# Eleven small parameter loads move from ScalarE's DMA queue to SyncE's, behind the first weight chunk, and TensorE runs five idle products instead of ten before x

## The chip, the cores and the metric

The kernel runs on one core of one Trainium2 chip. The metric is the device time of one execution in microseconds (us). Three runs of the kernel before took 1094.04 to 1094.62 us, median 1094.55 us. The profile is of one more execution, which took 1093.83 us.

Engines: PE is TensorE (PEld its weight loads), DVE is VectorE, ACT is ScalarE, POOL is GpSimd, SP is SyncE, which here only issues DMAs. ACT issues DMAs too, on a queue of its own.

## The reference

One layer of a hybrid encoder on 256 frames of 1024 numbers, all in float32. A normed copy of x is multiplied by `w_in`, and the product is split into a convolution branch, a state-space branch and two gates. After that comes a mixture of 32 experts, top 4 of each frame.

```python
h = rms_norm(x, norm_mix_g)
proj = h @ w_in                                   # 1024 x 3840
a_val, a_gate, u, g_conv, g_ssm = split(proj)
v = a_val * sigmoid(a_gate)
v = depthwise_causal_conv(v, conv_w) + conv_b     # 31 taps
y_conv = silu(layer_norm(v, conv_ln_g, conv_ln_b)) @ w_conv_out
y_ssm = s5_branch(u, ssm_a_re, ssm_a_im, ssm_log_step, b, c, ssm_d, w_ssm_glu, b_ssm_glu) @ w_ssm_out
x = x + (sigmoid(g_conv) * y_conv + sigmoid(g_ssm) * y_ssm) @ w_out
x = x + moe(rms_norm(x, norm_ffn_g))              # 32 experts: 1024 -> 2 x 1024 -> 1024
return rms_norm(x, norm_final_g)
```

The weights of all experts, some 400 MB, are read from HBM in every execution.

## The kernel before

Each engine has one program, written out in order; semaphores link them. The weights pass through a ring of 24 slots of 1 MB each in on-chip memory. SP issues every load of it in a fixed order, and before it fills a slot again it waits for the product that used the slot last. `w_in` comes in 15 chunks of 256 columns, the first one in two halves of 512 KB (L373, L374), the others whole (L369). After the mixer the ring holds the weights of two experts; each expert takes 12 slots, and its slots are filled again for the expert after next.

The start, with which the change deals, goes like this. SP issues x in two tiles of 128 frames (L362), then the gain of the first norm (L364, `norm_mix_g`, counted on the semaphore of x's second tile), then `w_in`. ACT issues eleven small loads at the same time: the convolution taps in two pieces (L648, semaphore `tap_in`), and nine rows or groups of rows of parameters (L649 to L654, semaphore `par_in`), all of them into rows of two on-chip tiles, `tap_rows` and `par_rows`. Then ACT loads the table for the square root (L656) and squares the two tiles of x (L659) for the norm's sums.

PE first multiplies the identity by itself ten times (L1367, `START_WARM`), into a bank that nobody reads. Then it transposes x's first tile, eight transposes (L1373), the gain (L1371), and x's second tile. DVE and ACT multiply the transposed x by the gain (L914, L665) into `hraw`. The first products with `w_in` (L1417 in `first_half`) run on this `hraw`, before the norm's divisor is known: four steps of k on the chunk's first half, then in the same instruction stream `spread_rstd` (two products, L1427, that spread the divisor over the partitions, and L1431, which transposes the 62 parameter rows), then four steps of k on the chunk's second half. L1431 waits for all nine parameter loads (`par_in`) and for a copy on POOL (L523) that itself waits for them. After `first_half` PE transposes the taps (L1466, waits for `tap_in`), and the rest of the projection follows (L1398), beside which DVE runs the convolution's taps.

PE issues in order: behind a waiting transpose everything else of PE waits. A float32 product stands in the trace as two instructions, so ten products are 20 records.

Of the kernel before, what the change touches and what calls it, by code (L numbers as in the profile page):

```python
# [33 lines left out]
W = 31  # L34
DS = 256
G, P, H = 16, 64, 16
ST = G * P // 128
# [21 lines left out]
MIDDLE = 4, 4, 4  # L59
END = {E - 3: (4, 2, 2, 2, 2), E - 2: (2, 2, 2, 2, 1, 1, 1, 1), E - 1: (2, 2, 2, 1, 1, 1, 1, 1, 1)}  # L60
WARM = 3, 4
START_WARM = 10
LEVELS = 8
BLOCK_STEPS = 16
AGAIN_STEPS = 6
# [4 lines left out]
def build(nc, x, norm_mix_g, w_in, conv_w, conv_b, conv_ln_g, conv_ln_b, w_conv_out,  # L70
# [3 lines left out]
    with ExitStack() as ctx:  # L74
# [3 lines left out]
        def sem(name):  # L78
            return ctx.enter_context(nc.semaphore(name))
# [4 lines left out]
        def at(slot, n, off=0):  # L84
            return ring[:, slot * CH + off:slot * CH + off + n]
# [98 lines left out]
        par_rows = ring[0:62, 12 * CH:12 * CH + 128]  # L184
        tap_rows = at(22, DC)[0:W, :]
# [22 lines left out]
        log_steps = ring[0:ST, 12 * CH + 1018:12 * CH + 1020]  # L208
# [6 lines left out]
        par_in = sem("par_in")  # L215
        tap_in = sem("tap_in")
# [143 lines left out]
        def _(sp):  # L360
# [5 lines left out]
            def load_win(c):  # L366
                if c >= WRING:
                    sp.wait_ge(win_pe, c - WRING + 1)
                sp.dma_start(grid(at(c % WRING, CH), KD, 256),  # L369
                             win_v[:, :, ORDER[c] * 256:ORDER[c] * 256 + 256]).then_inc(win_in[c % WRING], 16)  # L370

            win0, win0_v = grid(at(0, CH), KD, 256), win_v[:, :, ORDER[0] * 256:ORDER[0] * 256 + 256]
            sp.dma_start(win0[:, 0:4, :], win0_v[:, 0:4, :]).then_inc(win_in[0], 16)  # L373
            sp.dma_start(win0[:, 4:8, :], win0_v[:, 4:8, :]).then_inc(win0_late, 16)  # L374
            for c in range(1, WRING):
                load_win(c)
            for ri, src in enumerate((ssm_b_re, ssm_b_im)):
# [266 lines left out]
        def _(act):  # L644
            s = nc.scalar

            for r0, r1 in ((0, 16), (16, W)):
                act.dma_start(tap_rows[r0:r1, :], conv_w[0, r0:r1, :]).then_inc(tap_in, 16)  # L648
            act.dma_start(log_steps, ssm_log_step[0].rearrange("(t g) -> t g", g=2)).then_inc(par_in, 16)  # L649
            for src, r0 in ((ssm_a_re, 8), (ssm_a_im, 16)):  # L650
                act.dma_start(par_rows[r0:r0 + ST, :], src[0].rearrange("(t g) p -> t (g p)", g=2)).then_inc(par_in, 16)
            for src, r0, n in ((norm_ffn_g, 24, 8), (conv_b, 40, 6), (conv_ln_g, 46, 6), (conv_ln_b, 52, 6), (ssm_d, 58, 2),
                               (b_ssm_glu, 60, 2)):
                act.dma_start(par_rows[r0:r0 + n, :], src[0].rearrange("(k p) -> k p", p=128)).then_inc(par_in, 16)  # L654
            act.wait_ge(consts, 1)
            s.activation(neg_top, ident[:, 0:2], ACT.Sqrt)  # L656
            for t in range(TT):
# [705 lines left out]
        def _(pe):  # L1363
            mm, tr = nc.tensor.matmul, nc.tensor.transpose
            pe.wait_ge(consts, 1)
            for _ in range(START_WARM):
                mm(bank[6][:, 256:384], ident[:, :], ident[:, :], start=True, stop=True)  # L1367
# [496 lines left out]
```

## Time and profile before

| | |
|---|---|
| median of three runs | 1094.55 us |
| profiled execution | 1093.83 us |
| its span, first to last instruction | 1091.7 us |
| PE busy | 1054.1 us (97%) |
| DVE, ACT, POOL busy | 298.9, 151.3, 83.4 us |
| DMA engines, mean over the span | 395 GB/s |

The span leaves out 2.1 us of the profiled execution that lie before the first and after the last instruction. Times in the rows below are microseconds from the start of the span. In a row of the timeline, the first number is the start, the second how long the instruction or the run of like instructions took, and in brackets at the end stands how long the engine was idle before, and what ended that. "xN" is a count. A matmul's own duration includes its way through the array; how far apart the starts of two matmuls lie is the better measure of the rate.

### The profile page before, as it was taken

To read this page: it belongs to the slowest core of one execution; us is meant where nothing else is said; L and a number is where in the kernel's file an instruction comes from. 1 tells how busy PE (TensorE), PEld (TensorE's weight loads), DVE (VectorE), ACT (ScalarE), POOL (GpSimd) and SP (SyncE) were. 2 spreads that over 40 slices of the span, in tenths; PEclk is the share of its full clock that TensorE was granted. 3 is DMA by queue.
4 is the path that set the end of the run, shared out by engine and by line. 5 is a ranking of instruction groups with operands and counts; after the bars stand their busy time and mean duration, and the time that the engine had idled before them with its cause. 6 is when DMAs were issued, how large, how long until landed. Compare 5 with 4: busy or idle time off the path is not lost.

```text
span 1091.7 us, 12228 instructions
## 1 busy us (share of the span) xinstructions
PE 1054.1 (97%) x4978; PEld 456.8 (42%) x4979; DVE 298.9 (27%) x684; ACT 151.3 (14%) x276; POOL 83.4 (8%) x161
## 2 busy tenths in 40 slices
PE   9999999999999999999999999999999999999996
PEld 8888876333333333333333333333323333333332
DVE  5999843311111111111111111111111011111112
ACT  4111503101011111101010001100000000000003
POOL 3986100000000000000000000000000000000000
PEclk9999999999999999999999999999999999999999
DMA  9756786899999999999999999999999999999996
GB/s 284 232 167 256 316 349 255 343 428 434 430 430 435 430 433 431 432 432 432 431 433 431 428 431 428 435 430 432 432 432 432 432 430 433 431 433 424 425 424 249
DMA packets 43268, 431.48 MB, mean 395 GB/s; under 512 B 6773, under 2 KB 22443, under 8 KB 25482
## 3 DMA queue, kind: packets, MB, share of 16 engines
q1 hardware_dynamic: 42800, 430.48, 94.2%
q10 hardware_dynamic: 442, 0.64, 0.2%
q8 instruction: 18, 0.29, 0.1%
q14 instruction: 8, 0.07, 0.0%
HBM read 430.06 MB, written 1.05 MB: 395 GB/s over the span
## 4 chain that ended last, share of the span: by engine, by line
PE 71%; DMA 25%; ACT 1%; DVE 1%; issue 0%; another core or an unknown queue 0%; POOL 0%; SPq 0%; DVEq 0%; POOLq 0%
PE bank L1681 30%; DMA ring<-w_gate_up 23%; PE bank L1693 14%; PE bank L1398 9%; PE bank L1707 4%; PE bank L1619 3%; DMA ring<-w_down 3%; PE bank L1533 2%; PE bank L1561 2%; ACT area L788 1%; PE bank L1647 1%; PE bank L1672 1%; PE bank L1521 1%; PE bank L1575 1%; PE bank L1652 1%
## 5 line engine op out<-in xcount | busy, mean ns | idle before, releaser
L1681 PE MATMUL bank<-ring,area 128*64 128x512 f32 x2048 | 454.4, 600 | 18.8 <-DMA ring<-w_gate_up 18.8
L1681 PEld LDWEIGHTS bank<-ring,area 128*64 128x64 f32 x2048 | 149.9, 138 | 305.7 <-issue 268.4
L1693 PE MATMUL bank<-ring,area 128*64 128x512 f32 x1024 | 227.3, 595 | 5.6 <-ACT area L788 3.0
L1231 DVE TENSOR_SCALAR area<-bank 128x512 f32<-128x512 f32 x32 | 22.1, 692 | 668.6 <-PE bank L1681 668.6
L1693 PEld LDWEIGHTS bank<-ring,area 128*64 128x64 f32 x1024 | 71.7, 137 | 140.8 <-issue 132.9
L1398 PE MATMUL bank<-area,ring 128*128 128x256 f32 x464 | 102.3, 381 | 0.0
L1398 PEld LDWEIGHTS bank<-area,ring 128*128 128x128 f32 x464 | 87.5, 190 | 13.8 <-issue 1.8
L794 ACT ACTIVATE area<-area 128x512 f32<-128x512 f32 x32 | 20.1, 630 | 484.1 <-DVE area L1231 484.1
L1009 DVE SCALAR_TENSOR_TENSOR bank<-ring,spread,bank 128x256 f32<-128x256 f32 x174 | 71.5, 484 | 0.6
L1707 PE MATMUL bank<-area,spT 64*128 64x512 f32 x248 | 61.6, 615 | 0.7 <-ACT area L791 0.7
L1619 PE MATMUL bank<-rows,pick 128*64 128x512 f32 x256 | 62.2, 605 | 0.0
L791 ACT ACTIVATE area<-bank 128x512 f32<-128x512 f32 x32 | 19.1, 597 | 220.3 <-PE bank L1693 220.3
L1707 PEld LDWEIGHTS bank<-area,spT 64*128 64x128 f32 x248 | 21.3, 186 | 40.5 <-issue 38.9
L1647 PE MATMUL bank<-ident,area 128*128 128x128 f32 x256 | 36.8, 280 | 1.4 <-DVE area L1240 1.2
L1221 DVE TENSOR_TENSOR area<-bank,gain 128x512 f32<-128x512 f32 x31 | 21.4, 692 | 50.0 <-PE bank L1647 50.0
L1240 DVE TENSOR_TENSOR area<-area 128x512 f32<-128x512 f32 x32 | 34.2, 1067 | 1.1
L1619 PEld LDWEIGHTS bank<-rows,pick 128*64 128x64 f32 x256 | 15.5, 136 | 41.2 <-issue 41.0
L1647 PEld LDWEIGHTS bank<-ident,area 128*128 128x128 f32 x256 | 28.3, 141 | 5.8 <-DVE area L1240 1.5
L785 ACT ACTIVATE area<-bank 128x512 f32<-128x512 f32 x32 | 19.1, 598 | 75.8 <-PE bank L1619 75.8
L1237 DVE SCALAR_TENSOR_TENSOR area<-area 128x512 f32<-128x512 f32 x32 | 21.9, 685 | 0.0
L1234 DVE TENSOR_SCALAR area<-bank 128x512 f32<-128x512 f32 x32 | 21.8, 681 | 0.0
L1561 PE MATMUL bank<-ring 128*128 128x512 f32 x48 | 20.9, 592 | 0.0
(277 smaller groups left out, 513.4 us busy)
## 6 DMA issues: line engine op xcount, KB each, us to landing
ring<-w_gate_up SPq DMA_DIRECT2D x51, 4096.0 KB, 45.6
ring<-w_down SPq DMA_DIRECT2D x25, 4096.0 KB, 43.2
ring<-w_gate_up SPq DMA_DIRECT2D x26, 1024.0 KB, 8.8
ring<-w_gate_up SPq DMA_DIRECT2D x13, 2048.0 KB, 43.6
ring<-w_down SPq DMA_DIRECT2D x18, 1024.0 KB, 12.5
ring<-w_in SPq DMA_DIRECT2D x14, 1024.0 KB, 8.5
ring<-w_down SPq DMA_DIRECT2D x5, 2048.0 KB, 12.6
ring<-w_conv_out SPq DMA_DIRECT2D x1, 3072.0 KB, 13.1
```

The source lines that it names most:

```text
L1009: ins = v.scalar_tensor_tensor(conv[:, k, :] if w == W - 1 else acc, src, taps[:, k, w:w + 1], acc, ALU.mult, ALU.add)
L1231: return v.tensor_scalar(gc, bank[4][:, :], 7.0, None, ALU.min)
L1237: return v.scalar_tensor_tensor(lc, lc, 1.0, gc, ALU.add, ALU.mult)
L1240: return v.tensor_tensor(gc.rearrange("a (m p) -> a p m", p=128), grid(lc, 128, 4), grid(sg, 128, 4), ALU.mult)
L1398: last = mm(half_bank[n][m] if n < 2 else win_bank(n)[:, m * T:m * T + T], w[:, k, m * 128:m * 128 + 128], hT[:, k, :], start=(k == 0), st ...
L1533: last = mm(bank[4 + j][:, m * T:m * T + T], wconv[:, k, c:c + 128], silu[:, k, :], start=(k == 0), stop=(k == KC - 1))
L1561: return mm(bank[2 * t + h][:, :], gateC[:, k, t * 128:t * 128 + 128], wout[:, k, h * 512:h * 512 + 512], start=(k == 0), stop=(k == KD - 1))
L1619: last = mm(bank[6][64 * h:64 * h + 64, :], pick[:, t, :], rows[:, t, :].rearrange("a (p h m) -> a h p m", h=2, m=4)[:, h, :, :], start=(t ...
L1647: last = tr(bank[b][:, m * 128:m * 128 + 128], src[:, m * 128:m * 128 + 128], ident[:, :])
L1681: last = mm(bank[4 + b][64 * h:64 * h + 64, :], heT[:, k % 4, k // 4 * 64:k // 4 * 64 + 64], fours(w, b, h), start=False, stop=(k == KD - 1))
L1693: last = mm(bank[b][64 * h:64 * h + 64, :], src[:, k % 4, k // 4 * 64:k // 4 * 64 + 64], w[:, k % 2, h * 512:h * 512 + 512], start=(k == 0 ...
L1707: return mm(bank[n][:, :], by[r, n // 2, :], y[r, :], start=start, stop=stop, skip_group_check=True)
```

## The change

Two edits. The constant `START_WARM` goes from 10 to 5. And the eleven small loads are issued by SP, in the same order among themselves, after both halves of `w_in`'s first chunk and before its second chunk; ACT issues nothing at the start.

```diff
-START_WARM = 10
+START_WARM = 5
...
             sp.dma_start(win0[:, 0:4, :], win0_v[:, 0:4, :]).then_inc(win_in[0], 16)
             sp.dma_start(win0[:, 4:8, :], win0_v[:, 4:8, :]).then_inc(win0_late, 16)
+            for r0, r1 in ((0, 16), (16, W)):
+                sp.dma_start(tap_rows[r0:r1, :], conv_w[0, r0:r1, :]).then_inc(tap_in, 16)
+            sp.dma_start(log_steps, ssm_log_step[0].rearrange("(t g) -> t g", g=2)).then_inc(par_in, 16)
+            for src, r0 in ((ssm_a_re, 8), (ssm_a_im, 16)):
+                sp.dma_start(par_rows[r0:r0 + ST, :], src[0].rearrange("(t g) p -> t (g p)", g=2)).then_inc(par_in, 16)
+            for src, r0, n in ((norm_ffn_g, 24, 8), (conv_b, 40, 6), (conv_ln_g, 46, 6), (conv_ln_b, 52, 6), (ssm_d, 58, 2),
+                               (b_ssm_glu, 60, 2)):
+                sp.dma_start(par_rows[r0:r0 + n, :], src[0].rearrange("(k p) -> k p", p=128)).then_inc(par_in, 16)
             for c in range(1, WRING):
                 load_win(c)
...
-            for r0, r1 in ((0, 16), (16, W)):
-                act.dma_start(tap_rows[r0:r1, :], conv_w[0, r0:r1, :]).then_inc(tap_in, 16)
-            act.dma_start(log_steps, ssm_log_step[0].rearrange("(t g) -> t g", g=2)).then_inc(par_in, 16)
-            for src, r0 in ((ssm_a_re, 8), (ssm_a_im, 16)):
-                act.dma_start(par_rows[r0:r0 + ST, :], src[0].rearrange("(t g) p -> t (g p)", g=2)).then_inc(par_in, 16)
-            for src, r0, n in ((norm_ffn_g, 24, 8), (conv_b, 40, 6), (conv_ln_g, 46, 6), (conv_ln_b, 52, 6), (ssm_d, 58, 2),
-                               (b_ssm_glu, 60, 2)):
-                act.dma_start(par_rows[r0:r0 + n, :], src[0].rearrange("(k p) -> k p", p=128)).then_inc(par_in, 16)
             act.wait_ge(consts, 1)
             s.activation(neg_top, ident[:, 0:2], ACT.Sqrt)
```

The start of ACT's program before, from its first load to its first table; `ring` is the tile of 24 slots in which the parameter rows lie, and the two numbers are rows and columns:

```order
L648 DMA ring<-conv_w 16x768
L648 DMA ring<-conv_w 15x768
L649 DMA ring<-ssm_log_step 8x2
L651 DMA ring<-ssm_a_re 8x128
L651 DMA ring<-ssm_a_im 8x128
L654 DMA ring<-norm_ffn_g 8x128
L654 DMA ring<-conv_b 6x128
L654 DMA ring<-conv_ln_g 6x128
L654 DMA ring<-conv_ln_b 6x128
L654 DMA ring<-ssm_d 2x128
L654 DMA ring<-b_ssm_glu 2x128
L656 ACT_TABLE_LOAD
```

In the changed kernel none of these eleven loads is left on ACT, and the table load is its first work. SP's program of the changed kernel, from the row behind the first chunk's second half to the second chunk (line numbers are the changed kernel's; L369 is the same line in both):

```order
L376 DMA ring<-conv_w 16x768
L376 DMA ring<-conv_w 15x768
L377 DMA ring<-ssm_log_step 8x2
L379 DMA ring<-ssm_a_re 8x128
L379 DMA ring<-ssm_a_im 8x128
L382 DMA ring<-norm_ffn_g 8x128
L382 DMA ring<-conv_b 6x128
L382 DMA ring<-conv_ln_g 6x128
L382 DMA ring<-conv_ln_b 6x128
L382 DMA ring<-ssm_d 2x128
L382 DMA ring<-b_ssm_glu 2x128
L369 DMA ring<-w_in 128x8x256 x5
```

Before, the last row here stood directly behind L374, `w_in`'s first chunk; now eleven loads stand between. On PE only the count of products changes, ahead of x's transposes:

```order
 L1857 ISA
 L1362 UNCONDITIONAL_BRANCH
-L1367 MATMUL bank<-ident 128x128 x10
+L1367 MATMUL bank<-ident 128x128 x5
 L1373 MATMUL bank<-ident,rows 128x128 x8
 L1371 MATMUL bank<-ident,ring 128x8
```

Five products are gone, nothing else moves on PE; DVE's and POOL's programs are as they were.

## Rows read from the trace of the kernel before

**Rows 1.** The page, parts 1 and 4: busy time; the chain that ended last, by engine.
```profile
PE 1054.1 (97%) x4978; PEld 456.8 (42%) x4979; DVE 298.9 (27%) x684; ACT 151.3 (14%) x276; POOL 83.4 (8%) x161
...
PE 71%; DMA 25%; ACT 1%; DVE 1%; issue 0%; another core or an unknown queue 0%; POOL 0%; SPq 0%; DVEq 0%; POOLq 0%
```

**Rows 2.** SP's queue, first 300 us: who waited for whom, total us, times, longest.
```profile
SPq L402 <- PE bank L1681: 57.9, 16, 10.3
```

**Rows 3.** DVE, first 140 us: who waited for whom, same columns.
```profile
DVE area L1071 <- PE bank L1501: 2.4, 1, 2.4
```

**Rows 4.** Timeline of all engines, first 30 us: start, us, engine, line, what.
```profile
0.79 0.86 SPq L362 DMA_DIRECT2D rows<-x  x2
0.80 1.13 ACTq L648 DMA_DIRECT2D ring<-conv_w  x2
...
1.57 4.64 PE L1367 MATMUL bank<-ident 128*128 128x128 f32 x20 [1.57 <-POOL ident L517]
...
2.12 0.40 SPq L373 DMA_DIRECT2D ring<-w_in  x1
...
2.57 0.53 SPq L374 DMA_DIRECT2D ring<-w_in  x1
...
4.91 0.28 ACTq L654 DMA_DIRECT2D ring<-b_ssm_glu  x1
...
6.00 1.59 PE L1373 MATMUL bank<-ident,rows 128*128 128x128 f32 x8
...
6.62 1.04 ACT L659 ACTIVATE ring<-rows 128x1024 f32<-128x1024 f32 x1
...
7.52 0.22 PE L1371 MATMUL bank<-ident,ring 8*128 8x8 f32 x1
...
7.67 1.09 PE L1373 MATMUL bank<-ident,rows 128*128 128x128 f32 x8
...
8.22 0.69 DVE L914 TENSOR_TENSOR ring<-bank,area 128x512 f32<-128x512 f32 x1 [0.28 <-PE bank L1373]
...
9.06 1.97 PE L1417 MATMUL bank<-ring 128*128 128x256 f32 x8 [0.30 <-DVE ring L914]
...
9.86 0.28 POOL L523 COPY ring<-ring 8x128 f32<-8x128 f32 x1 [8.20 <-DMA ring<-b_ssm_glu]
...
11.40 0.27 PE L1431 MATMUL bank<-ident,ring 62*128 62x62 f32 x1
...
11.60 1.99 PE L1417 MATMUL bank<-ring 128*128 128x256 f32 x8
...
14.01 16.24 PE L1398 MATMUL bank<-area,ring 128*128 128x256 f32 x74
```

**Rows 5.** DMA issues, whole span: size of each, median us from issue to landing.
```profile
rows<-x SPq DMA_DIRECT2D x2, 512.0 KB, 4.1
...
out<-ring ACTq DMA_DIRECT2D x1, 512.0 KB, 3.3
...
ring<-ssm_c_im SPq DMA_DIRECT2D x1, 64.0 KB, 2.6
```

**Rows 6.** Line L373, first half of the first chunk: issue to landing.
```profile
DMA to landing us min/median/max: 6.2/6.2/6.2
```

**Rows 7.** DMA issues from 3.0 to 3.5 us: second chunk, and first chunk's second half.
```profile
ring<-w_in SPq DMA_DIRECT2D x1, 1024.0 KB, 9.6
ring<-w_in SPq DMA_DIRECT2D x1, 512.0 KB, 7.4
```

**Rows 8.** Stretches: length, busy us of PE, PEld, DVE, ACT, POOL, clock, DMA share, GB/s.
```profile
2.00:4.00 2.00, 2.00 (x11) 2.00 (x11) 0.00 (x0) 0.00 (x0) 0.00 (x0) 1.00 0.81 266
4.00:6.00 2.00, 2.00 (x12) 2.00 (x11) 0.00 (x0) 0.78 (x1) 0.00 (x0) 1.00 1.00 332
```

**Rows 9.** Line L1681 in two stretches: PE, PEld busy, granted clock, DMA share, GB/s.
```profile
747.80:751.20 3.40, 3.40 (x12) 0.95 (x10) 0.50 1.03 443
751.20:754.60 3.40, 3.40 (x20) 1.11 (x18) 1.00 1.01 434
```

## The prediction

> **What bounds the kernel now.** I read the page first: PE is busy 97% of the span, and the chain that ended last is 71% PE and 25% DMA [rows 1]. The DMA part lies in the second half, where the experts' weights stream. That stream starts early or late with PE all the same, since SP's refills wait for PE's products: 57.9 us in the first 300 us, for the experts' first product alone [rows 2]. Next the start, in the timeline. From 1.57 us on PE hardly pauses; the last pause is the 0.30 us before the first product with `w_in` at 9.06, and from 14.01 the projection runs unbroken [rows 4]. DVE, PE's rival in the mixer, is the one that waits where they meet: 2.4 us for L1501 [rows 3]. So I take what PE gains or loses before 14.01 as passed on to the end one to one.
>
> The change touches only these first 14 us. Its size is bounded by how much of them is not forced.
>
> **Five products less.** The ten products are 20 records in 4.64 us, 0.21 to 0.23 us each, from 1.57 [rows 4]; ten records less end them at about 3.9 instead of 6.2. PE transposes x's first tile from 6.00. That tile was issued at 0.79 and takes 4.1 us [rows 4, 5]: there at 4.9. So today's products cover a tile that has landed, for 1.1 us.
>
> The second tile, with the norm's gain behind it, has no landing of its own in the rows. Lower bound: issued at about 1.2, plus 4.1, is 5.3. Upper bound: L1371, which waits for both, runs at 7.52. By 6.0 us 2 x 266 + 2 x 332 KB = 1.2 MB had moved [rows 8], and x with the convolution's taps is 1.05 + 0.10 MB, so the last byte lay near 5.8, and I take 6.5 for its landing and the gain's. The taps, 95 KB, no longer share the way: 0.3 us less at 332 GB/s, for x and for `w_in`. So the first tile is there at 4.6 and the second at 6.2 to 6.5. Eight transposes at today's early rate of 0.21 us take 1.7 us, 4.6 to 6.3: L1371 runs at 6.5 instead of 7.52, 1.0 us earlier.
>
> **What is late next.** From L1371 to DVE's L914 are 0.70 us today, and L914 takes 0.69 us [rows 4]: 6.5 + 0.7 + 0.7 = 7.9, up to 8.2 if the transposes run slow. The first half of `w_in`'s chunk lands at 2.12 + 6.2 = 8.3 [rows 4, 6], less 0.3 without the taps. So the first product starts near 8.3 instead of 9.06: 0.3 us of the gain is gone, 0.75 us left.
>
> From there to L1431 PE needs 11.40 - 9.06 = 2.34 us [rows 4]; it would come to it at 10.65. L1431 needs the parameters.
>
> **Eleven loads behind the chunk.** ACT issues them from 0.80 to 5.19, 4.4 us [rows 4]. On SP they start behind L374, at 3.10, and end at about 7.5, the last issue starting at 7.2. The landing of the last one is not in the trace of before. From below: a small load with little ahead of it took 2.6 us [rows 5], so 9.8. From above: today POOL's copy, which waits for them, starts 4.95 us after the last issue (4.91 to 9.86, rows 4), so 12.15. Between them lies the queue itself: they stand behind the second half of the chunk, which lands at 2.57 + 7.4 = 10.0 [rows 4, 7], less 0.3 without the taps beside it, plus 0.3 for the taps now ahead and 0.2 for the small rows. I take 10.2, the row that they queue behind. POOL's copy then ends at 10.6, and L1431 can run at 10.7 to 10.9 instead of 11.40. At 12.15 it would run at 12.6, 1.2 us late, with all of PE behind it.
>
> The Trainium skill ("DMA: Bandwidth & Descriptors", section "Queues, rings and completion order") says that a DMA engine takes turns between the rings that have work and takes the descriptors of one ring in order. It speaks against this edit: on a ring of their own the parameters got turns beside `w_in`, on SP's they get none before it is through; that agrees with the 10.2 above, which the rows gave.
>
> So the gain is 0.5 us at L1431 and stays so: the second four steps start 0.5 us earlier (today 11.60), their half of the chunk is there by 10.0, L1466 and L1398 follow.
>
> **Costs hidden.** The second chunk is issued at 7.5 instead of 3.1. Today it lands at 3.1 + 9.6 = 12.7 [rows 7]; the bytes ahead of it are the same, SP's queue still holds two microseconds of work when it joins, so 12.7 to 13.0, and L1398 wants it at 13.5. This cover is 0.5 us thick; if it fails, its loss is what the chunk is late. ACT's table load and squares come up to 2 us earlier (the first square stands at 6.62 today, behind the issues); nobody waited for them, worth nothing. At the end ACT's queue is used for the first time, for the output's half of 512 KB, 3.3 us today [rows 5]; if a first use costs, I bound it by 0 and the 0.7 us by which that load exceeds the 2.6 us of a small one.
>
> **The sum.** 1093.8 - 0.5 for the profiled execution, which is 0.7 us under the median; some of it is lost to the clock (below), so 0.4 us off the median of 1094.55: 1094.15, say 1094.2.
>
> **The clock, the main risk.** Today the products keep PE at work from 1.57, and the rate rises among the transposes: eight take 1.59 us from 6.00, the next eight 1.09 us [rows 4]. That the two rates are the half and the full clock is seen later, where the granted clock is 0.50 (1.2 of 2.4 GHz) and 12 products of L1681 fit in 3.40 us, against 20 at 1.00 [rows 9]. Before the rise PE had been at work since 1.57 without a pause. After the change it works 2.3 us, pauses 0.7 us for x, and works on from 4.6; whether the rise comes as early, no row says. At half clock the eight records of L1417 take 3.4 us, not 1.7 us, and L1427 0.4 us more. My forecast has the rise before or early among L1417's records; each record at half costs 0.21 us, and the first one or two are in the 0.1 us that I took off.
>
> **Rivals.**
> Rival 1, the pause sets the rise back into the first eight records of L1417. With four of them at 0.43 us from 8.4, the other four at 0.216 us, they end at 11.0, L1427 at 11.5: L1431 0.1 us late instead of 0.5 us early; with three to six at half, 0.1 us early to 0.5 us late. For it: nothing in the trace shows a rise with a pause ahead of it. Against: the pause is short. Time: 1094.4 to 1095.0.
>
> Rival 2, slower: the clock rises only behind L1431, because the work that raises it begins again with the products at 8.4, the transposes ahead of them doing nothing for it. Eight records at half end at 11.8, L1427 at 12.7, L1431 at 13.0; with two records of the second eight at half and six at full the end is 15.2 against 13.6 now: 1.6 us slower, 1096.2. It decides from the point where about four of the first eight run at half. If the rise were later still, all sixteen and L1427 at half cost up to 2.8 us, 1097.4. Against: today the rate rose in the middle of transposes. For: the 4.4 us before those were products.
> The Trainium skill ("TensorE: Matmul & The Clock Gate", section "Part 4: PE-mode transpose") states the rule behind this rival: a transpose doesn't count as PE being busy in the way a matmul does. This trace doesn't settle it; no run here shows a rise after transposes alone.
>
> Rival 3, the parameters land at 12.15, as long after their issue as now: L1431 1.2 us late, 1095.8. For: they land slowly today too. Against: today they share turns with 2 MB.
>
> Rival 4, more gain: x and the parameters land at their lower bounds and the clock is up: the full 0.75 to 1.0 us, 1093.6.
>
> **How the numbers follow.** Forecast (1093.8 to 1094.6) 0.45; rival 1 0.25; rival 2 0.15; rival 3 0.08; rival 4 0.07. Leaving out the top of rival 2 and the bottom of rival 4, the range is 1093.4 to 1096.2. A measurement of this kernel can tell about 0.2%, 2.2 us, from no change. Faster by more needs 2.2 us from a start that gives 1 us at most: 0.03. Slower by more is the upper part of rival 2, or a failed cover I don't see: 0.07. The same: 0.90.
>
> **What would show it.** Right: the first transpose near 4.6 to 4.9, L1417 near 8.3, POOL's L523 near 10.3, L1431 near 10.9, L1398 near 13.5, and the rest shifted by the same. L1417's starts 0.43 us apart mean rival 1 or 2; L523 after 11 means rival 3. Wrong altogether: a shift at 14 us that the end doesn't show, or a pause of PE before L1398 for the second chunk.

## The result and the profile after

The changed kernel takes 1095.79 us in the median of 22 runs (1093.74 to 1098.52), the kernel before beside it 1094.04 us (22 runs, 1093.29 to 1097.13). The ratio is 1.0014, 95% interval 1.0008 to 1.0020, so the change costs 0.9 to 2.2 us. The forecast was 1094.2, a gain of 0.4. The profiled execution took 1096.18 us, its span 1094.3. What follows is from its trace; the lines answer to those of [rows 4], POOL's copy is L531 now.

```profile
0.79 1.28 ACT L656 ACT_TABLE_LOAD   x1 [0.66 <-PEq L1857]
...
1.57 2.50 PE L1367 MATMUL bank<-ident 128*128 128x128 f32 x10 [1.57 <-POOL ident L525]
...
4.20 1.06 ACT L659 ACTIVATE ring<-rows 128x1024 f32<-128x1024 f32 x1 [1.90 <-DMA rows<-x]
...
4.22 1.59 PE L1373 MATMUL bank<-ident,rows 128*128 128x128 f32 x8
...
5.76 0.22 PE L1371 MATMUL bank<-ident,ring 8*128 8x8 f32 x1
...
7.14 0.25 SPq L382 DMA_DIRECT2D ring<-b_ssm_glu  x1
...
7.44 9.80 SPq L369 DMA_DIRECT2D ring<-w_in  x5
...
8.16 1.99 PE L1417 MATMUL bank<-ring 128*128 128x256 f32 x8 [1.15 <-DMA ring<-w_in]
...
12.06 0.30 POOL L531 COPY ring<-ring 8x128 f32<-8x128 f32 x1 [10.39 <-DMA ring<-b_ssm_glu]
...
12.51 0.24 PE L1431 MATMUL bank<-ident,ring 62*128 62x62 f32 x1 [1.91 <-POOL ring L531]
...
12.68 1.99 PE L1417 MATMUL bank<-ring 128*128 128x256 f32 x8
...
14.60 0.55 PE L1466 MATMUL bank<-ident,ring 31*128 31x31 f32 x6
...
15.08 1.13 PE L1398 MATMUL bank<-area,ring 128*128 128x256 f32 x4
```

Read it down PE's column. The transposes come 1.78 us earlier (4.22, was 6.00), the first product with `w_in` 0.90 us earlier (8.16, was 9.06) at the full rate. Then PE stands still for 1.91 us at L1431: POOL's copy waited until 12.06 for the last parameter load, `b_ssm_glu`. The projection begins at 15.08, 1.07 us later than before.

The chain that ended last names the wait itself; in before the chain had only work of PE from 9.06 to 20 us:

```profile
2.56 0.50 SPq L374
3.11 0.50 SPq L376
4.46 0.55 SPq L379
7.14 4.78 DMA ring<-b_ssm_glu
12.75 1.92 PE bank L1417 x8
```

It runs through SP's issues and one load of 1 KB, 4.78 us from its issue at 7.14 to its count at 11.92. That the loss passes to the end is read from an activation of the experts, 32 times in each kernel (first and last start, before and then after):

```profile
L785 ACT ACTIVATE area<-bank x32: 597/597/600, 193.6 to 1047.1; 128x512 f32<-128x512 f32 x32
```

```profile
L785 ACT ACTIVATE area<-bank x32: 597/598/601, 194.7 to 1048.4; 128x512 f32<-128x512 f32 x32
```

The shift is 1.1 us at 194 us and still 1.3 at the end. The medians lie 1.75 us apart; 1.07 us of it is there when the projection begins, behind the wait at L1431, and the rest no run separates from the scatter of single executions.

### The profile page after: what moved, and what is told of

It reads as the page before. It is cut to its first block, busy times and chain, and to the rows that moved or that the text cites. A ratio compares the mean times of both kernels' runs of the same rounds, so it can differ in the third digit from the quotient of the medians.

```text
span 1094.3 us, 12208 instructions
## 1 busy us (share of the span) xinstructions
PE 1052.8 (96%) x4968; PEld 454.2 (42%) x4969; DVE 298.9 (27%) x684; ACT 151.7 (14%) x276; POOL 83.4 (8%) x161
## 4 chain that ended last, share of the span: by engine, by line
PE 66%; DMA 30%; ACT 1%; DVE 1%; SPq 1%; issue 0%; another core or an unknown queue 0%; POOL 0%; DVEq 0%; POOLq 0%
PE bank L1681 28%; DMA ring<-w_gate_up 27%; PE bank L1693 12%; PE bank L1398 9%; DMA ring<-w_down 3%; PE bank L1707 3%; PE bank L1619 3%; PE bank L1533 2%; PE bank L1561 2%; ACT area L788 1%; PE bank L1647 1%; PE bank L1672 1%; PE bank L1521 1%; PE bank L1575 1%; PE bank L1652 1%
## 5 line engine op out<-in xcount | busy, mean ns | idle before, releaser
L1681 PE MATMUL bank<-ring,area 128*64 128x512 f32 x2048 | 454.4, 600 | 18.9 <-DMA ring<-w_gate_up 18.9
L1681 PEld LDWEIGHTS bank<-ring,area 128*64 128x64 f32 x2048 | 149.6, 138 | 306.3 <-issue 269.3
L1398 PE MATMUL bank<-area,ring 128*128 128x256 f32 x464 | 102.3, 381 | 0.0
L1398 PEld LDWEIGHTS bank<-area,ring 128*128 128x128 f32 x464 | 87.5, 190 | 13.8 <-issue 1.8
## 6 DMA issues: line engine op xcount, KB each, us to landing
ring<-w_down SPq DMA_DIRECT2D x18, 1024.0 KB, 14.2
ring<-w_down SPq DMA_DIRECT2D x5, 2048.0 KB, 14.1
```

Of the source, the lines that this page charges most:

```text
L1398: last = mm(half_bank[n][m] if n < 2 else win_bank(n)[:, m * T:m * T + T], w[:, k, m * 128:m * 128 + 128], hT[:, k, :], start=(k == 0), st ...
L1681: last = mm(bank[4 + b][64 * h:64 * h + 64, :], heT[:, k % 4, k // 4 * 64:k // 4 * 64 + 64], fours(w, b, h), start=False, stop=(k == KD - 1))
```

## The experiments

The expectations name their theories by letters. **Q**: the parameters are late because they queue on SP behind `w_in`, and L1431 waits. **C**: the clock, set back by the shorter run of products, is the loss. **L**: the last load lands a fixed time after its own issue. **E**: the small rows cost the DMA engines time on any queue. B, F, R, D, P and N are explained in the expectations that use them; the N of e5 is another than that of e17 and e18. "Before" is always the kernel before, run on the same chip beside the experiment.

**Five products alone (e1).** From the kernel before: `START_WARM = 5`, the loads stay on ACT.

> Only the five products are taken away; the eleven loads stay on ScalarE's queue. Theory Q (the loss is the parameters' landing: on SyncE's ring they stand behind w_in's first chunk, and each small row holds up its ring some 0.15 us): L523 stays near 9.9 us, L1431 comes at 10.4 to 10.7 us instead of 11.40, L1398 near 13.1 us, the time is 0.6 to 0.9 us under before. Rival C (the loss comes from the products: with a pause ahead of x the clock rises later in most executions than in the one profiled): the first L1417 records stand 0.43 us apart or the time varies, and the median is 1.0 to 1.7 us over before.

Measured: 1094.71 us, ratio 1.0002 (0.9993 to 1.0011).

```profile
4.91 1.97 PE L1373 MATMUL bank<-ident,rows 128*128 128x128 f32 x8 [0.84 <-DMA rows<-x]
...
8.83 2.35 PE L1417 MATMUL bank<-ring 128*128 128x256 f32 x8
...
11.55 0.27 PE L1431 MATMUL bank<-ident,ring 62*128 62x62 f32 x1
...
14.16 16.02 PE L1398 MATMUL bank<-area,ring 128*128 128x256 f32 x73
```

No measurable change, and neither theory's time. The transposes begin 1.1 us earlier, but all sixteen run at the slow rate (1.97 us for eight), and so do the first records of L1417. Its eight records start at

```
8.83 9.27 9.69 9.94 10.15 10.37 10.58 10.80
```

The first two steps are 0.44 and 0.42 us, the others 0.21 to 0.25. The trace's records of the granted clock begin at 9.7 us in this execution; in before they begin at 7.1, among the transposes. So here the rate of PE, which rises later, eats the gain, and L1431 comes 0.15 us late. That is the sign which C and the prediction's rival 1 named, in one execution, at a small price.

**The loads alone (e2).** From the changed kernel: `START_WARM = 10`.

> Only the eleven loads move to SyncE; ten products stay. Theory Q: L523 starts at 12.0 to 12.2 us, L1431 at 12.5, L1398 at 15.1, as in the changed kernel, and the time is 1.0 to 1.5 us over before. Rival C: the time is that of before, within 0.4 us, whatever L523 does.

Measured: 1095.54 us, ratio 1.0010 (1.0001 to 1.0019).

```profile
8.79 1.97 PE L1417 MATMUL bank<-ring 128*128 128x256 f32 x8 [0.29 <-DVE ring L914]
...
11.97 0.33 POOL L531 COPY ring<-ring 8x128 f32<-8x128 f32 x1 [10.31 <-DMA ring<-b_ssm_glu]
...
12.44 0.24 PE L1431 MATMUL bank<-ident,ring 62*128 62x62 f32 x1 [1.24 <-POOL ring L531]
...
15.02 15.16 PE L1398 MATMUL bank<-area,ring 128*128 128x256 f32 x69
```

With all ten products the loss is there in full: L1398 at 15.02, 1.01 us late. Q stands, and C is not the changed kernel's loss.

**The changed kernel once more.** Does the loss hang on when the rate of PE rises?

> The changed kernel once more, for a second profile. Theory Q: L523 at 11.9 to 12.2, L1431 at 12.4 to 12.6 and L1398 at 15.0 to 15.2 again, wherever the clock rises. Rival C (the profile was a lucky one for the clock): L1417's first records 0.43 us apart and L1398 at 15.3 or later.

Measured: 1094.68 us in this one execution.

```profile
4.17 1.97 PE L1373 MATMUL bank<-ident,rows 128*128 128x128 f32 x8
...
6.27 1.95 PE L1373 MATMUL bank<-ident,rows 128*128 128x128 f32 x8
...
8.27 1.99 PE L1417 MATMUL bank<-ring 128*128 128x256 f32 x8
...
12.61 0.24 PE L1431 MATMUL bank<-ident,ring 62*128 62x62 f32 x1 [1.91 <-POOL ring L531]
```

Here all sixteen transposes ran at the slow rate (in the first profile 1.59 and 1.09 us), the products at the fast one, and the wait is the same 1.91 us. For the changed kernel C is out a second time.

**Only the taps on SP (e3).** Five products, taps behind the chunk on SP, the nine parameter loads on ACT.

> Five products; the two pieces of convolution taps go to SyncE behind w_in's first chunk, the nine parameter loads stay on ScalarE. Theory Q: the parameters keep their turns beside w_in and start 1.1 us earlier on their queue: L523 starts at 9.0 to 9.9 us, L1431 at 10.3 to 10.7, the taps land by 10.5 us where L1466 wants them at 12.5, and the time is 0.6 to 1.0 us under before. Rival C: as for the five products alone, 1.0 to 1.7 us over before.

Measured: 1094.39 us, ratio 1.0000 (0.9991 to 1.0008).

```profile
10.37 0.28 POOL L525 COPY ring<-ring 8x128 f32<-8x128 f32 x1 [8.71 <-DMA ring<-b_ssm_glu]
...
10.79 0.24 PE L1431 MATMUL bank<-ident,ring 62*128 62x62 f32 x1
...
13.58 16.67 PE L1398 MATMUL bank<-area,ring 128*128 128x256 f32 x76
```

L1398 comes 0.43 us earlier than before: close to what I forecast for the whole change, but too little to show in the time. Q's copy (9.0 to 9.9) and its time (0.6 to 1.0 us under before) were missed. So the loss needs the nine parameter loads on SP; what the taps ahead of them add to it, e16 shows.

**The parameters between the halves of the chunk (e4).** From the changed kernel: the nine loads stand ahead of L374, the taps behind it.

> The changed kernel, but the nine parameter loads are issued by SyncE between the two halves of w_in's first chunk, the taps behind the second half. Theory Q: with 512 KB less ahead of them the parameters land near 9.6 us, L523 starts at 9.7, L1431 near 10.3, but the chunk's second half lands 1 to 1.5 us later (11 to 11.5 us) and PE waits for it: L1398 near 13.8 to 14.1, the time within 0.4 us of before. Rival L (a small load on SyncE's queue takes 4.8 us from its issue to its landing, wherever it stands): last issue at 5.6, L523 starts at 10.4 to 10.6. Rival C: 1.0 to 1.7 us over before.

Measured: 1096.52 us, ratio 1.0015 (1.0006 to 1.0024).

```profile
9.38 0.28 POOL L531 COPY ring<-ring 8x128 f32<-8x128 f32 x1 [7.72 <-DMA ring<-b_ssm_glu]
...
11.01 1.99 PE L1417 MATMUL bank<-ring 128*128 128x256 f32 x8 [0.61 <-DMA ring<-w_in]
...
15.26 14.90 PE L1398 MATMUL bank<-area,ring 128*128 128x256 f32 x60 [1.77 <-DMA ring<-w_in]
```

The last load is issued at 5.32 and counted at 9.24: 3.9 us, against 4.8 in the changed kernel, so L's fixed time is refuted; Q's direction holds (the copy moves with the transfer ahead). The kernel is still no faster, because the second chunk, issued at 7.07, lands at 15.22, and PE waits 1.77 us for it at L1398 (Q had 13.8 to 14.1). The cover that I called 0.5 us thick is gone. Then, behind this pause, the granted clock fell:

```profile
15.59:19.00 3.41, 3.41 (x10) 2.69 (x9) 1.59 (x10) 2.58 (x6) 0.45 (x4) 0.50 1.09 348
19.00:22.00 3.00, 3.00 (x15) 2.65 (x14) 1.17 (x3) 0.79 (x2) 2.61 (x15) 1.00 1.09 348
```

Ten products in 3.41 us at 0.50 (1.2 GHz), then fifteen in 3.00 at 1.00: 10 products would have taken 2.0 us, so I estimate that this fall cost 1.4 us more.

**The transposition of the parameters later (e11).** From the changed kernel: L1431 with its waits stands behind the second four steps.

```diff
-                pe.wait_ge(par_in, 16 * 9)
-                pe.wait_ge(ls_rows, 1)
-                tr(bank[7][:, 0:62], par_rows[:, :], ident[0:62, 0:62]).then_inc(params_pe, 1)
...
+            pe.wait_ge(par_in, 16 * 9)
+            pe.wait_ge(ls_rows, 1)
+            tr(bank[7][:, 0:62], par_rows[:, :], ident[0:62, 0:62]).then_inc(params_pe, 1)
```

> The changed kernel, but PE's transposition of the parameters (L1431) stands behind the second four steps of first_half, not ahead of them. Theory Q (PE's loss is its wait at L1431 alone): the second eight records of L1417 start at 10.5 to 10.8 us instead of 12.68, L1431 comes at 12.4 to 12.6, and the next bound is w_in's second chunk, which lands at 14.2: L1398 at 14.2 to 14.4 instead of 15.08 (14.01 in the kernel before), time 0.2 to 0.5 us over before. Rival: DVE or ACT hold the start back as well, L1398 stays at 14.8 to 15.1 and the time at 1.0 to 1.5 us over before.

Measured: 1094.64 us, ratio 1.0005 (0.9996 to 1.0014).

```profile
10.53 1.89 PE L1417 MATMUL bank<-ring 128*128 128x256 f32 x8
...
13.13 0.24 PE L1462 MATMUL bank<-ident,ring 62*128 62x62 f32 x1 [0.71 <-POOL ring L531]
13.78 0.53 PE L1466 MATMUL bank<-ident,ring 31*128 31x31 f32 x6 [0.41 <-ACT spread L670]
...
14.84 15.38 PE L1398 MATMUL bank<-area,ring 128*128 128x256 f32 x70 [0.54 <-DMA ring<-w_in]
```

The products no longer wait (10.53, 12.68 in the changed kernel), and the time can't be told from before any more; but nor can it from the changed kernel, whose interval overlaps. L1398 still comes 0.83 us late, at the rival's 14.8 and not at Q's 14.2 to 14.4. The parameters were counted at 12.57 this time, and the transposition (now L1462) waits 0.71 us for them; L1466 waits 0.41 us for ACT's copy of them, and L1398 0.54 us for the second chunk, which lands at 14.80. So taking L1431 out of the products' way is not enough: the taps' transposition stands behind the same parameters, and the second chunk is the next wait.

**Other orders on ACT (e5, e6, e10).** All three have eight products and the loads on ACT: e5 otherwise as before; e6 the nine parameters first and the taps behind them; e10 the taps behind ACT's square root instead.

> The kernel before with eight idle products in place of ten, all loads on ScalarE. They end at 5.0 us, when x's first tile lands (4.9), so PE has no pause ahead of x. Theory P (the pause is what delays the clock's rise): transposes start at 5.0 to 5.2, the rise comes as in the kernel before, L1417 at 8.3 to 8.5, L1431 at 10.7 to 10.9 (before 11.40), L1398 at 13.3 to 13.5, the time 0.4 to 0.7 us under before. Rival N (the rise varies from execution to execution whatever stands ahead of x): L1431 anywhere from 10.7 to 11.6 and the median within 0.3 us of before.

> As with eight products, and ScalarE issues the nine parameter loads ahead of the taps, not behind them. Theory Q (small rows held up by what stands ahead of them on their own ring, and taking turns beside w_in): parameters land by 9.0 us instead of 9.72, L523 at 9.0 to 9.3, x's tiles 0.2 us earlier since the taps come later, L1431 at 10.4 to 10.7, L1398 at 13.0 to 13.2; the time 0.6 to 1.0 us under before. Rival: L523 stays at 9.9 and nothing is won over eight products alone.

> The kernel before with eight idle products; ScalarE issues the nine parameter loads first and the two pieces of taps only behind the square root of the norm (L661). Theory Q: parameters take turns beside w_in and have no taps ahead of them, x's tiles land at 4.2 and 5.8 us; L1371 at 6.4, L1417 at 8.2 to 8.5, L523 at 9.5 to 10.3, L1431 at 10.6 to 11.0, the taps land by 12.5 where L1466 wants them at 12.6 to 13.0, L1398 at 13.1 to 13.5: 0.5 to 0.9 us under before. Rival: the parameters or the second chunk land late here too (L523 after 10.6, the chunk after 13.6), and nothing is won.

Measured: e5 1093.99 us, ratio 1.0002 (0.9993 to 1.0011), L1398 at 13.77; e6 1094.40, ratio 1.0004 (0.9995 to 1.0013), L1398 at 14.12; e10 1095.66, ratio 1.0015 (1.0006 to 1.0024), L1398 at 15.46. e5 and e6 can't be told from before, and the gains that P and Q forecast for the three did not come. e5 loses 0.38 us to `w_in`, and its L1417 take 2.33 us behind ACT's late squares: the fifth record starts at 9.65, 0.45 us behind the fourth. In e6 the first half of `w_in` lands at 8.82, and the parameters are counted at 9.45 (Q: by 9.0). In e10 the taps are issued at 8.40 on ACT's queue, where the last parameter row passes at 9.37; their own first packet passes at 12.28 and the last count comes at 14.93, 6.5 us behind the issue, and PE waits 1.71 us for them at L1466. Why their packets start so late no run shows; a queue other than `w_in`'s was no remedy for a late issue.

**More rows (e8, e9).** Eight more loads of eight rows, in e8 on SP ahead of the second chunk, in e9 (the kernel before) on ACT behind its loads.

> The changed kernel with eight more loads of 8 rows of 512 bytes on SyncE, behind the parameters and ahead of w_in's second chunk; nobody waits for them early. Theory Q (each small load holds up its ring by some 0.16 us, and what stands behind waits for the slowest ring): the second chunk lands 1.2 to 1.5 us later than in the changed kernel (14.2 us), at 15.4 to 15.7, and L1398 starts when it lands; L523 stays at 12.0 to 12.2. Rival B (only the bytes count: 32 KB, 0.1 us): the second chunk lands at 14.2 to 14.5, L1398 at 15.1.

> The kernel before with the same eight more loads on ScalarE, behind its parameters. Theory Q (the hold-up is of the ring, and w_in has SyncE's): the second chunk lands at 12.6 to 13.0 as before (12.7), L1398 at 14.0 to 14.3. Rival E (the hold-up is of the DMA engine, whatever the ring): the second chunk lands at 13.8 to 14.2.

Measured: one execution each, 1098.32 and 1098.40 us. In e8 the second chunk lands at 15.7, as Q said, but not because of bytes. The stretches of [rows 8], 9 to 12 us, of e8 and then of before:

```profile
9.00:10.00 1.00, 1.00 (x6) 0.90 (x5) 0.16 (x1) 0.67 (x2) 0.00 (x0) 1.00 0.31 85
10.00:11.00 1.00, 0.68 (x6) 0.46 (x4) 0.00 (x0) 0.28 (x1) 0.00 (x0) 1.00 0.05 11
11.00:12.00 1.00, 0.00 (x0) 0.00 (x0) 0.80 (x3) 0.10 (x1) 0.12 (x1) 1.00 0.47 73
```

```profile
9.00:10.00 1.00, 0.94 (x4) 0.87 (x5) 0.96 (x4) 0.97 (x4) 0.14 (x1) 1.00 1.10 350
10.00:11.00 1.00, 1.00 (x7) 0.89 (x6) 0.22 (x1) 0.69 (x2) 0.80 (x5) 1.00 1.09 348
11.00:12.00 1.00, 1.00 (x8) 0.79 (x7) 0.01 (x1) 0.49 (x2) 0.69 (x5) 1.00 1.09 348
```

The last two numbers are the engines' busy share and GB/s. Here the DMA engines have next to nothing to do while SP issues small loads (0.25 to 0.55 us each): the chunk is issued only at 9.95 (7.44 in the changed kernel). And the parameters are counted at 11.74 although the DMA engines are nearly idle around them: their lateness isn't bandwidth. In e9 the chunk lands at 13.36 (before: 12.70), between Q's and E's numbers; ACT, issuing until 7.96, loads its table at 8.00. The products wait 2.71 us behind its late work, behind that pause the granted clock is 0.50 from 13.0 to 16.4, and the projection starts at 18.11, 4.1 us later than before.

**Fewer loads, same rows (e13).** Four parameter loads become one of 20 rows.

> The changed kernel with six parameter loads in place of nine: the rows of conv_b, conv_ln_g, conv_ln_b and ssm_d come in one load of 20 rows from w_out, so these parameters are not the reference's. Theory Q (each small load on the ring takes some 0.17 us in series behind w_in's chunk): POOL's copy of the log steps starts 0.4 to 0.6 us earlier than in the changed kernel (12.06), at 11.4 to 11.7. Rival L (4.8 us from the last issue, which comes 1.0 us earlier): at 11.0 to 11.2. Rival B (the chunk's bytes alone): at 12.0.

Measured: 1095.88 us in one execution, copy at 11.87, L1431 at 12.52. The last of six loads, issued at 6.26, is counted at 11.74, hardly before the last of nine (11.92). Q and L missed, B's 12.0 came nearest, and I took it that the number of loads doesn't matter. That was too quick, as the next runs showed.

**What the time behind the chunk consists of (e14, e15, e16).** The trace keeps every packet of a load and every count that it adds to its semaphore. In the changed kernel the last packet of the parameter rows is done at 9.74, ahead of the 10.2 at which I had put the landing; their 54 counts, one for each row, come in from 10.05 to 11.92. So the data pass quickly, and the counting is slow. F: a fixed time. R: a price per row. D: loads standing one behind another on the first of the DMA engines.

e14, from the changed kernel (all nine likewise; POOL fills the tile with a constant first):

```diff
-                sp.dma_start(par_rows[r0:r0 + n, :], src[0].rearrange("(k p) -> k p", p=128)).then_inc(par_in, 16)
+                sp.dma_start(par_rows[r0:r0 + 2, :], src[0].rearrange("(k p) -> k p", p=128)[0:2]).then_inc(par_in, 16)
```

> The changed kernel, but each of the nine parameter loads brings only two rows (18 rows in all, not 54); the other rows hold a constant that POOL writes at the start, so most parameters are not the reference's. In the changed kernel the trace has all packets of these rows done by 9.74, yet their counts on the semaphore come in one after another from 10.05 to 11.92, and with the 31 tap rows ahead of them from 8.67: 85 rows in 3.25 us, 0.038 us a row. Theory R (each row is counted about 0.038 us behind the one before, whatever load it is of): 31 + 18 rows take 1.9 us from 8.7, the last at 10.6, so POOL's copy L533 starts at 10.5 to 10.9, L1431 at 10.9 to 11.4. Theory F (a fixed time, 1.4 to 2.3 us behind the landing of w_in's second half): L533 at 11.4 to 12.3. Theory D (what counts is how many loads stand one behind another on the first of the 16 engines, eleven as before): L533 at 11.5 to 12.1.

e15, in place of the eight loads behind `log_steps`:

```diff
+            for r0, r1 in ((8, 32), (40, 62)):
+                sp.dma_start(par_rows[r0:r1, :], w_out[0, r0:r1, 0:128]).then_inc(par_in, 16)
```

> The changed kernel, but the parameter rows come in three loads instead of nine (eight rows of steps, then 24 and 22 rows, which are rows of w_out in place of the parameters): the same 54 rows and bytes, and SP is done with the issue some 2 us earlier. Theory R (0.038 us a row): 85 rows as before, the last one counted at 11.6 to 12.2, POOL's copy there. Theory F (fixed time behind w_in's second half): 11.4 to 12.3. Theory D (loads behind one another on the first engine, now seven instead of eleven deep, 3.25 us by 7/11 = 2.1 from 8.7): 10.8, copy at 10.6 to 11.1. The second chunk is issued near 5 us and lands before 13.3 by every theory.

e16 issues the two tap loads on ACT.

> The changed kernel, but the two loads of taps are issued by ACT at the start, as in the kernel before; the nine parameter loads stay on SP behind w_in's second half. Theory R (0.038 us a row): 54 rows instead of 85 behind the chunk, 2.05 us from 8.7: the last counted at 10.8, POOL's copy L531 at 10.6 to 11.1, L1431 at 11.1 to 11.5, as late as before the change; time within 0.5 us of the kernel before, 1093.7 to 1094.7. Theory F: copy at 11.4 to 12.3, L1431 1 us late, 1095.3 to 1095.9. Theory D: nine deep instead of eleven, copy at 11.2 to 11.5, 1094.9.

Measured (one execution each of e14 and e15, of which only the start is read, since later work depends on the parameters' values); POOL's copy in e14, e15, e16:

```profile
10.71 0.47 POOL L534 COPY ring<-ring 8x128 f32<-8x128 f32 x1 [8.65 <-DMA ring<-b_ssm_glu]
```

```profile
11.77 0.42 POOL L528 COPY ring<-ring 8x128 f32<-8x128 f32 x1 [10.11 <-DMA ring<-w_out]
```

```profile
11.37 0.28 POOL L529 COPY ring<-ring 8x128 f32<-8x128 f32 x1 [9.70 <-DMA ring<-b_ssm_glu]
...
11.80 0.24 PE L1431 MATMUL bank<-ident,ring 62*128 62x62 f32 x1 [0.43 <-POOL ring L529]
```

e16 took 1094.51 us, ratio 1.0003 (0.9993 to 1.0012). For POOL's copy R had e14 and e15 right and e16 wrong, D only e16, F only e15. None holds as put. In e16 L1398 starts at 14.38, 0.37 us later than before: with the two tap loads out of the way most of the changed kernel's loss is gone, though the nine loads stay on SP. In e15 the second chunk, issued at 5.38, should have landed before 13.3 by every theory, and landed at 13.95. But the 18 counts of e14 show a pattern, in us from the span's start:

```
9.06 9.08 | 9.24 9.26 | 9.42 9.43 | 9.60 9.61 | 9.79 9.81 | 9.98 10.00 | 10.20 10.20 | 10.37 10.40 | 10.54 10.57
```

Nine pairs for nine loads of two rows, each pair 0.17 to 0.22 us behind the last, while all their packets were done by 8.38.

**The number of loads alone (e17, e18).** As e14, with three and with six of the nine loads left. N: each load is counted a fixed time behind the one before, whatever its rows.

> As the run with two rows a load (e14), but only three of the nine parameter loads are left (6 rows); POOL's constant stands for the rest, so most parameters are not the reference's. In e14 the counts came in pairs, nine pairs 0.19 us apart, the last 2.2 us behind the last packet (8.38 to 10.57); with 54 rows in three loads (e15) 1.26 us, in six loads (e13) 1.82. Theory N (each load is counted 0.15 to 0.2 us behind the one before, whatever its rows): the last count 1.1 to 1.4 us behind the last packet, three pairs 0.19 apart. Theory F (a fixed time behind the last packet of small rows): 1.8 to 2.3 us. Theory R (per row): 6 rows, 0.9 to 1.1 us.

> The same with six of the nine loads (12 rows); most parameters are not the reference's. Theory N: the last count 1.5 to 1.8 us behind the last packet, six pairs 0.19 us apart. Theory F: 1.8 to 2.3 us. Theory R (0.035 us a row, from 0.9): 1.2 to 1.4 us.

Measured: POOL's copy in e17, then e18:

```profile
9.88 0.28 POOL L531 COPY ring<-ring 8x128 f32<-8x128 f32 x1 [7.82 <-DMA ring<-b_ssm_glu]
```

```profile
11.22 0.41 POOL L531 COPY ring<-ring 8x128 f32<-8x128 f32 x1 [9.16 <-DMA ring<-b_ssm_glu]
```

All runs together, by the trace's records of packets and counts; the last column is the time from the last packet of a parameter row to its last count:

```
kernel                          loads  rows  last packet  last count  between
before (ACT's queue)              9     54      8.84         9.72       0.88
changed                           9     54      9.74        11.92       2.18
changed, again                    9     54      9.79        11.84       2.05
e2, ten products                  9     54      9.64        11.83       2.19
e11, transposition later          9     54     10.32        12.57       2.25
e16, taps on ACT                  9     54      9.15        11.23       2.08
e4, between the halves            9     54      7.52         9.24       1.72
e14, two rows each                9     18      8.38        10.57       2.19
e13                               6     54      9.92        11.74       1.82
e18, two rows each                6     12      9.32        11.08       1.76
e15                               3     54     10.37        11.63       1.26
e17, two rows each                3      6      8.27         9.74       1.47
```

Behind the chunk nine loads take 2.05 to 2.25 us, six 1.8, three 1.3 to 1.5, with 54 rows or with 6: the time goes with the number of loads, not with the rows (one execution each). F and R fall; N holds in the steps of e14 and e18 (0.17 to 0.22 us) and in e18's total, but e17's six counts show no such pairs, and N misses its total by 0.07 us; F misses e18's only by 0.04, but e17's by 0.33. e13 had hidden the effect because in it the packets themselves were done 0.2 us later.

Why the same nine loads take less on ACT's queue (0.88 us in before, 0.58 to 1.09 in e1, e3, e5, e6 and e10) stays open. They are issued at like distances there, but in before their packets pass from 5.7 to 8.8, in the changed kernel from 9.07 to 9.74, in one burst; with packets apart, no load need stand behind another's counts. e4, whose packets pass from 6.32 to 7.52, has 1.72 us, which fits; e11, from 8.22 to 10.32, has 2.25, which doesn't, and the records don't say which DMA engine a packet was on.

## Why the prediction was wrong

The step that failed is the sum for the parameters' landing: "I take 10.2, the row that they queue behind", with 0.2 us "for the small rows". The packets were through at 9.74, earlier than that. But there was no term for the counts of nine loads, which on SP's queue come in one behind another: 2.2 us, last count 11.92. Against before the last count is 2.20 us later; 0.90 of it is the packets (9.74, was 8.84) and 1.30 the counting (2.18, was 0.88). The counting was in no view that I read, because on ACT's queue the same nine loads show 0.9 us of it. Rival 3 had the right event and nearly its size, POOL's copy at 12.15 against 12.06, but I gave it 0.08, taking the turns shared with `w_in` for the reason of today's slow landing. Its reason, "as long after their issue as now", isn't what holds either: 4.78 us in the changed kernel, 3.9 in e4, 5.5 in e13. That its 1095.8 meets the measured 1095.79 is luck: it stands on the old median of 1094.55, and the kernel before measured 1094.04 beside the changed one. The result lies in my range only because the rivals reach there; the way of the change, faster, was wrong.

Point by point:

- Products: right that they only covered the wait for x. The first transpose came at 4.22 (I said 4.6 to 4.9), since x's first tile no longer shares the way with the taps (4.91 in e1, which leaves them on ACT, 4.23 in e3).
- Second tile: L1371 at 5.76 against my 6.5; L1417 at 8.16 against 8.3, waiting for `w_in` as said. The 0.3 us off for `w_in`, though, were 0.24 us for the first half (8.35 to 8.11) and nothing for the second (9.94 to 9.97).
- ACT's earlier squares, "worth nothing": right with PE as late as before, wrong behind a PE that is early. In e5, where ACT still issues, the eight L1417 take 2.33 us instead of 1.99.
- The second chunk: said 12.7 to 13.0, landed 14.22. My "SP's queue still holds two microseconds of work" counted bytes; the DMA engines ran at 218 GB/s from 9 to 10 us where they had moved 350. SP's later issue alone doesn't explain it: in e15 the chunk is issued at 5.38 and lands at 13.95, in e14, with two rows a load, it is issued at 7.15 and lands at 12.80. So for the chunk the rows seem to count too; no run separates the two. In the changed kernel L1431's wait hides this; in e4 and e11 it is the next wait.
- Clock: in the changed kernel rivals 1 and 2 didn't happen. In both of its profiles L1417 runs at the fast rate, in one of them right behind sixteen transposes at the slow rate. But the risk was there: in e1 the first two steps of L1417 are slow (0.44 and 0.42 us), which was rival 1's sign. In the traces of all runs the records of the granted clock begin at 5.7 to 7.1 us where eight or ten products run first (six traces), at 5.3 to 9.7 where five do (thirteen). By the rule of the Trainium skill that stood beside rival 2 ("TensorE: Matmul & The Clock Gate", "Part 4: PE-mode transpose"), transposes do not count as PE being busy in the way matmuls do. Rival 2's price, a rise only behind L1431 (12.51), was seen in none of these traces.
- End: right that the shift at 14 us passes on (1.07 us there, 1.1 at 194 us), and that a gain or loss here stays near 0.2% of the time. But the interval of 22 runs reaches 0.06% to either side, finer than the 0.2% that I took.
- The rule of the Trainium skill on queues that I weighed ("DMA: Bandwidth & Descriptors", "Queues, rings and completion order") is that a DMA engine takes the descriptors of one ring in order. The packets agree as far as the records go: in the changed kernel the taps' pass from 7.94 us, the parameter rows' behind them from 9.07. The order says nothing of how long the counts take, and the 2.2 us could not have come out of it.

None of the versions beats the kernel before measurably; the best, e3, has a ratio of 1.0000.

## What to carry to other kernels

When many small loads are put behind one another on a queue, count them, not their bytes: here each cost 0.25 to 0.55 us of the issuing engine and about 0.1 to 0.2 us more until the last count was in, and the wait for the last one paid for all. Before a load moves to another queue, ask which instruction waits for its last count, and what stands behind that instruction in its engine's order: here a transposition of 0.24 us held up two microseconds of products that didn't need it, and moving it behind them brought the projection only 0.24 us forward in e11's profile, because the next instructions waited for the same parameters and for the next chunk. A gain at the front of a chain is worth no more than the slack up to the next wait.

## What the runs showed of the hardware

- A small load is done in two steps that can lie 2 us apart: its packets, and its counts. Nine two-row loads behind one another were counted in steps of 0.17 to 0.22 us (e14).
- Small loads ahead of a chunk cost the DMA engines rate: eleven took it from 350 to 218 GB/s between 9 and 10 us, at a busy share of 0.93 (was 1.10). Nineteen took it to 11 GB/s between 10 and 11 us, at a share of 0.05: there the engines had next to no work while SP was issuing.
- The slow rate of PE at the start ends where the trace's records of the granted clock begin, at 1.00: at 7.1 us in before, 5.3 in the changed kernel, 8.1 when it ran again, 9.7 in e1. At these times the transposes' starts go from 0.21 to 0.11 us apart (in before and the changed kernel), and L1417's in e1 from 0.43 to 0.21; in the second execution it is the time between the last transpose and L1417. Ahead of the first record the trace has none, and the views show 1.00 there all the same, in [rows 8] too. So they do for the changed kernel run again, 4 to 8 us, with the eight transposes from 4.17 and from 6.27 in 1.97 and 1.95 us:

```profile
4.00:6.00 2.00, 1.91 (x9) 1.57 (x8) 0.00 (x0) 1.65 (x3) 0.00 (x0) 1.00 0.80 247
6.00:8.00 2.00, 2.00 (x10) 1.75 (x9) 1.10 (x4) 0.78 (x4) 0.00 (x0) 1.00 1.06 363
```

That the slow rate of the start is the half clock is an inference from the factor of two in these starts, in the prediction too. When it ends differs between executions of one kernel (5.3 and 8.1 us in the changed one).
